# Late modulation products of a two-block mixer stack: eight half units at the entry of the gated scan instead of two

## The reference, cut to what matters

```python
c_act = jax.nn.silu(c)
for layer in range(2):
    mod = c_act @ w_ada[layer] + b_ada[layer]          # 1024 x 3072
    shift, scale, gate = mod[:, :D], mod[:, D:2*D], mod[:, 2*D:]
    h = _modulated_norm(x, norm_g[layer], shift, scale)
    ...                                                # layer 1 also: mkv = c_act @ w_ada_kv + b_ada_kv
    x = x + gate * y
```

```python
L = jnp.where(strict, einsum(k_beta, k) * decay, 0.0); a_mat = L + eye(64)
sol = triangular_solve(a_mat, rhs)                      # per head and chunk
attn = jnp.where(tril, einsum(q, k) * decay, 0.0)
...
_, o = lax.scan(step, S0, ...)                          # over the 8 chunks
```

## Time and profile before

| | us |
|---|---|
| median of 3 runs | 1232.59 |
| lowest and highest | 1232.29, 1235.76 |
| the profiled execution | 1230.61 |
| its span (first to last instruction) | 1228.7 |
| TensorE busy in the span | 1176.3 (96%) |
| VectorE, ScalarE, GpSimd busy | 487.4, 538.8, 370.7 |

### The profile page before, as it was taken

The page is one execution under the profiler, slowest core; times in us unless marked ns, Lnnn a source line. Parts: engine busy times, 40 slices in busy tenths (PEclk is TensorE's granted clock), DMA queues, the critical chain, the costliest instruction groups (busy, mean ns, idle before and its releaser), DMA issues.

```text
span 1228.7 us, 21193 instructions
## 1 busy us (share of the span) xinstructions
PE 1176.3 (96%) x8874; PEld 914.7 (74%) x8874; DVE 487.4 (40%) x919; ACT 538.8 (44%) x924; POOL 370.7 (30%) x148
## 2 busy tenths in 40 slices
PE   5999999999989999999999999999999999999998
PEld 3788886677668888777765666888887777777767
DVE  4575544544324472341314553640202332231462
ACT  4232237633336343543547774333125433754430
POOL 0143343132265314344331001332144122333250
PEclk8999999999999999999999999999999999999999
DMA  9723331356650232322422100323132321324201
GB/s 318 231 69 102 102 101 37 103 188 223 208 180 2 69 103 70 102 81 91 129 69 73 26 14 1 124 89 103 34 106 84 111 78 35 103 70 155 87 1 69
DMA packets 105761, 121.14 MB, mean 99 GB/s; under 512 B 5145, under 2 KB 91705, under 8 KB 105673
## 3 DMA queue, kind: packets, MB, share of 16 engines
q1 hardware_dynamic: 101424, 116.14, 29.9%
q10 hardware_dynamic: 4248, 3.73, 1.1%
HBM read 111.47 MB, written 2.10 MB: 92 GB/s over the span
## 4 chain that ended last, share of the span: by engine, by line
PE 84%; ACT 6%; DVE 4%; issue 3%; DMA 1%; ACTq 0%; SPq 0%; POOL 0%; DVEq 0%
PE ps L2039 42%; PE ps L2846 4%; PE ps L2644 3%; PE ps L2635 2%; PE ps L2180 2%; PE ps L2085 2%; PE ps L2426 2%; PE ps L2669 2%; PE ps L2648 1%; PE ps L2778 1%; PE ps L2123 1%; PE ps L2203 1%; PE ps L2256 1%; PE ps L2731 1%; PE ps L2453 1%
## 5 line engine op out<-in xcount | busy, mean ns | idle before, releaser
L604 POOL TENSOR_TENSOR wlo<-raw,whi 128x2048 fp32r<-128x2048 f32 x53 | 245.1, 4624 | 586.1 <-ACT whi L768 571.5
L768 ACT ACTIVATE whi<-raw 128x2048 fp32r<-128x2048 f32 x52 | 99.3, 1911 | 203.2 <-PE ps L2039 164.2
L610 POOL TENSOR_TENSOR wlo<-raw,whi 128x2048 fp32r<-128x2048 f32 x10 | 46.4, 4641 | 111.0 <-ACT whi L857 62.7
L1277 ACT ACTIVATE p<-sc,nmx 128x256 f32<-128x256 f32 x64 | 32.0, 501 | 49.6 <-PE ps L2765 29.5
L857 ACT ACTIVATE whi<-raw 128x2048 fp32r<-128x2048 f32 x11 | 21.1, 1918 | 62.7 <-PE ps L2039 62.7
L2039 PE MATMUL ps<-hC_hi,whi 128*128 128x512 f32 x184 | 47.1, 398 | 0.8 <-POOL wlo L604 0.8
L1861 DVE CUSTOM_DVE_ANT_0 sc<-ps,biast 128x256 f32<-128x256 f32 (+1 forms) x64 | 23.1, 394 | 62.2 <-PE ps L2756 33.3
L2039 PE MATMUL ps<-hC_lo,whi 128*128 128x512 f32 x184 | 45.5, 390 | 0.0
L2039 PE MATMUL ps<-hC_hi,wlo 128*128 128x512 f32 x184 | 45.4, 389 | 0.0
L2039 PEld LDWEIGHTS ps<-hC_hi,whi 128*128 128x128 f32 x184 | 33.8, 188 | 14.9 <-issue 6.4
L2039 PEld LDWEIGHTS ps<-hC_lo,whi 128*128 128x128 f32 x184 | 34.5, 188 | 7.4
(11 more groups left out here) (514 smaller groups left out, 2822.5 us busy)
## 6 DMA issues: line engine op xcount, KB each, us to landing
raw<-in_w_in_dram SPq DMA_DIRECT2D x24, 1024.0 KB, 5.2
raw<-in_w_in_a_dram SPq DMA_DIRECT2D x16, 1024.0 KB, 5.8
raw<-in_w_ada_dram SPq DMA_DIRECT2D x8, 1024.0 KB, 5.5
late_w<-in_w_ada_dram SPq DMA_DIRECT2D x8, 1024.0 KB, 5.5
raw<-in_w_kv_dram SPq DMA_DIRECT2D x8, 1024.0 KB, 5.1
raw<-in_w_in_b_dram SPq DMA_DIRECT2D x8, 1024.0 KB, 5.3
ada_a<-in_w_ada_dram SPq DMA_DIRECT2D x4, 1024.0 KB, 10.0
ada_b<-in_w_ada_dram SPq DMA_DIRECT2D x4, 1024.0 KB, 13.2
```

The lines of the kernel that those rows point to most:

```text
L604: pool.tensor_tensor(wlo[:, s, :], raw[:, s, :], whi[:, s, :].bitcast(F32), ALU.subtract).then_inc(lo_ready, 1)
L610: pool.tensor_tensor(wlo[:, s, :], raw[:, s, :], whi[:, s, :].bitcast(F32), ALU.subtract).then_inc(lo_ready, 1)
L768: A(whi[:, s, :], raw[:, s, :], ACT.Copy).then_inc(hi_ready, 1)
L1277: A(p2[:, n % 2, 256 * e:256 * e + 256], sc2[:, n % 2, 256 * e:256 * e + 256], ACT.Exp, scale=-1.0, bias=nmx[:, grp, t, 2 * hp + e:2 * hp ...
```

## The change

The first `filler` call moves three halves between `keys_keys` and `keys_queries`, and the one behind `keys_queries` takes five halves instead of two. Nothing else is edited, but `fill` is one list, so every later call takes halves that stand six places further on. The list is empty after the middle call of level 3 in pair 3. The end call of level 3, both calls of level 4 in pair 3 and the `filler(len(fill))` behind it find nothing: these are six halves (one, one, two and two).

```diff
             for h in range(2):
                 keys_keys(h)
+            filler(3)
             for h in range(2):
                 keys_queries(h)
-            filler(2)
+            filler(5)
             for p in range(HG // 2):
                 nxt = 2 * p + 2 if p < HG // 2 - 1 else None
                 for lv, b in enumerate(LEVELS):
```

## The result

The changed kernel took 1227.15 us (median of 6 runs, 1224.91 to 1227.95) beside 1232.92 us for the kernel before (1231.27 to 1237.54). The ratio is 0.9948, with an interval of 0.9928 to 0.9969: 5.8 us faster. The kernel before was 1.4 us slower in the first set (1232.92) than in the second (1231.53), and the second rests on more runs (10 and 14), so 3.3 us is the safer figure. The profiled execution took 1226.95 us with a span of 1225.0, 3.7 us less than before.

What follows compares the result with a forecast made beforehand. TensorE, busy for 1176.3 of 1228.7 us, was taken to bound the kernel. Gains of 1.5 (clock), 2.2 (end of pair 3) and 0.7 (pauses) summed to 4.4 us, giving 1228.2 us, range 1225.0 to 1233.0.

Steps and rivals of the forecast that it cites:

- The halves at the entry cost nothing: Around the key-query products: three halves ahead and five behind fit TensorE's idle time, cost 0, with 0.3 and 1.6 us spare.
- The slack of the loads: At the entry: both `late_w` loads, issued by 235.3, have landed two microseconds before 244.5, when first wanted.
- The clock, 1.5 us: Behind the entry: less idle time keeps the clock up for 28 matmuls; 1.5 us gained, from 0 to 1.6.
- The end of pair 3, 2.2 us: Levels 3 and 4 to the recurrence in pair 3: six empty calls give 0.1 + 0.0 + 0.5 + 1.5, taken as 2.2 us.
- the columns to be last before the recurrence: End of pair 3: columns with VectorE's addition need 1.02 us, ScalarE's taking out of w 0.81, so the columns stay last.
- The pauses, 0.7 us: TensorE's instruction waits, 245 to 350 us: shifted block borders and fewer late loads gain 0.7 us net, within 4 us either way.
- The sum, 4.4 us: Whole kernel: clock 1.5, end of pair 3 2.2 and pauses 0.7 give 4.4 us, a forecast of 1228.2 us.
- More pauses at the entry: Rival: four loads in a row at the entry make two more instruction portions late; 1.7 us gained, 1230.9 us; chance 0.20.
- The clock falling all the same: Rival: 1.6 us idle before the first level still drops the clock; only 2.9 us gained, 1229.7 us; chance 0.14.
- Slower: Rival: instruction blocks late in nearly all levels 2 to 4, eight more late; 5 us slower, 1237.7 us; chance 0.06.

Runs made afterwards that it cites:

- all_ahead: The changed kernel with all eight halves ahead of the key-query products and none behind; 1231.69 us, ratio 1.0004 to the kernel before.
- tail_only: The changed kernel with the six halves moved to the entry left out there but for three small matmuls; 1230.71 us, ratio 0.9996 to the kernel before.
- small_loads_before: The kernel before with late weight loads and the first output projection's load cut to an eighth; 1222.85 us beside 1231.53.
- after: The changed kernel itself, first set and first profile; 1227.15 us, ratio 0.9948 to the kernel before.
- after_again: The changed kernel measured once more, unedited, on another occasion; 1228.28 us beside 1231.53, ratio 0.9973 to the kernel before.
- even: The changed kernel with one half instead of two at the end of level 4 in every pair; 1227.56 us, ratio 0.997 to the kernel before.
- small_loads_after: The changed kernel with late weight loads and the first output projection's load cut to an eighth; 1217.39 us beside 1231.53.
- small_loads_clock: The kernel before with six spare halves in the entry's idle time and weight loads cut to an eighth; 1220.23 us, ratio 0.9904 to the kernel before.
- half_loads: paced with every late unit loaded by two 512 KB transfers instead of one of 1 MB; 1230.72 us, ratio 0.9987 to the kernel before.
- half_even: half_loads with one half instead of two at the end of level 4 in every pair; 1228.67 us, ratio 0.9978 to the kernel before.
- clock_only: The kernel before with six spare halves added in TensorE's idle time at the entry, all real halves unmoved; 1232.01 us beside 1231.22, ratio 1.000.
- paced: The changed kernel with the four loads at the entry spread out, three waiting for products of levels 0 and 1; 1230.93 us, ratio 0.9994 to the kernel before.
- ten: even with ten halves at the entry and one half instead of two ending levels 0 and 1 of pair 0; 1226.4 us beside 1231.53, ratio 0.9963.

## Why the prediction was right, step by step

**The halves at the entry cost nothing:** right. The three ahead end with 0.46 us to spare (0.3 predicted), the five behind leave 1.86 us (1.6 predicted). The slack of the loads was overrated: the text read 6 GB/s at 242 us as landed. It was the tail of a load. In the kernel before, the second of the two `late_w` loads was issued at 234.72 and landed 9.4 us later, at 244.1, where the first took 5.3 us. In all_ahead its half units waited until 244.88. In the changed kernel its load landed after 9.3 us, at some 244.4, and its half units came at 245.8; they did not wait, but it was a matter of a microsecond.

**The clock, 1.5 us:** right in size, too sure in kind. Where it holds, the distance from product to product is 3.59 us against 5.19, 1.6 us. Over all profiles:

| idle before the first level | profiles | the clock there, and the distance from product to product |
|---|---|---|
| 3.00 to 4.16 us | before, tail_only, small_loads_before, all_ahead | fell in all four, 5.0 to 6.3 us |
| 1.85 to 1.86 us | after, after_again, even, small_loads_after, small_loads_clock, half_loads, half_even | held, 3.58 to 3.59 us |
| 1.85 to 1.86 us | clock_only, paced | fell, 5.18 us |
| under 1 us, in one piece | ten | held, 3.58 us |

So the eight halves make the fall at the entry rare, not impossible, and where it falls without them it can cost 2.7 us as well as 1.6. What decides at 1.86 us stays open; full loads alone do not, for it held and fell with them.

The prediction had the clock down at the entry only, which was so in the kernel before. In five of the ten other profiles with full loads it fell in the levels too, each time behind a pause called issue:

| profile | pause before the fall | granted clock 0.50 within |
|---|---|---|
| after_again | 1.90 us | 256 to 260 us |
| clock_only | 2.25 us | 339 to 343 us |
| even | 1.60 us | 320 to 324 us |
| half_loads | 2.09 us | 277 to 281 us |
| paced | 2.10 and 2.25 us | 277 to 282 and 342 to 347 us |

The eleven profiles with full loads have 21 pauses of 1.5 to 2.5 us in the levels. Behind six of them the clock fell, behind 15 it held, one of 2.50 us among these. A fall cost 1.3 to 2.2 us, by the estimate from distance and waits. So a pause can cost nearly twice its length, and the sum of the pauses alone does not tell what they cost.

**The end of pair 3, 2.2 us:** right. Behind the w products 1.6 us came (1.5 predicted), ahead of them 0.5 (2.13 us from the last second product to w before, 1.63 after), and the middle call of level 4 gave nothing, since VectorE's 0.55 us took its place. One link was wrong: the text held the columns to be last before the recurrence, and by the chain it is ScalarE's taking out of w. ScalarE ends at 352.63 us and VectorE's addition of the columns at 352.62, so the two end together.

**The pauses, 0.7 us:** not borne out. The sum fell by 0.9 us in the first profile (8.4 to 7.5) and rose by 0.8 in the second (9.2), so that the first came near the forecast was luck. Nor did it fall for the reason given. In pair 3 there was to be one pause or less instead of 1.56 and 1.28 us. There are two, of 2.25 and 0.72 us, 3.0 in all after 2.8: the output weight's loads, now issued at 332.18 and 338.14, stand where the first falls. Levels 3 and 4 do run with the DMA at rest, from 342.75 on, as the text had it. The second pause stands in level 3 all the same: it ends at 344.91, and its 16 KB packet had moved at 342.5, with the end of the last load. This sum ranges from 4.8 to 10.0 us over the profiles with full loads, which is as much as the whole effect. What sets it in a given execution, no edit here controlled. The text bounded its change by 4 us on both sides, and all profiles lie within that.

**The sum, 4.4 us:** in the trace the recurrence came 3.96 us sooner after the key-key products (116.51 and 112.55 us). The terms measured give 1.6 + 1.6 + 0.5 + 0.9 = 4.6. Of the 0.6 us too many, 0.3 is a wait for VectorE before a second product (at 332.38) that the kernel before does not show; the rest is not assigned. In the second profile it came only 0.8 us sooner. In the runs it was 5.8 and 3.3 us, on both sides of the forecast's 4.4. The median of 1227.15 us is 1.1 below the forecast. The terms of the clock and of pair 3 were right; that the whole came out so near owes something to the pauses.

**The rivals.** More pauses at the entry: seen in after_again, 1.90 us and a fall of the clock behind it. The clock falling all the same: seen in clock_only and paced. Executions of both kinds may be what makes the second set 2.5 us poorer than the first; that is not shown. Slower: not seen with this change.

**Open:** clock_only and tail_only each gave nothing in the times (1.000, 0.9996), while the whole change gave 0.27 to 0.52%, and with small loads the parts give 2.6 and 2.8 us. The clock_only profile shows how that can be: the clock fell at the entry all the same and once more in the levels. For tail_only the profile does not show it; it was the fastest run of its set. The likeliest reading is that each part shifts the blocks of instructions against the loads in its own way and lost its 2 us in pauses and in falls of the clock behind them. That is argued from the range of both; one profile for each kernel cannot show it. Open too is which pauses the clock outlasts.

## What to carry to other kernels

Idle time of the bounding engine ahead of a dense stretch costs twice, once as idle and once as a low clock behind it; spare work belongs there first, in front of the waits that it fits under (three ahead, five behind) and not all in one place. Work taken off the end of a loop is worth what is late next, here 2.1 us for 3.2 us of halves. When small matmuls stream beside large loads, take the loads away once to see what they cost: here 9 to 11 us of 1230, some 7 of them as pauses for instructions, more than any reordering moved. And read the granted clock over the whole stretch, not only at the place of the edit.

## What was not expected of the hardware

- A pause of TensorE for instructions depends on the bytes that the DMA moves beside it: with 2.4 to 2.8 MB instead of 20.9 in 100 us the pauses went from 8.4 and 7.5 us to 0.9 and 0.5; halving the single transfers changed nothing (7.8 us). All 58 such pauses of 0.5 us or more end 2.2 to 2.8 us after a 16 KB packet of the instruction queue has moved.
- The same matmuls behind the same 1.86 us of idle TensorE kept the full clock in seven profiles and lost it in two. In the levels it fell behind six of 21 pauses of 1.5 to 2.5 us; it fell behind one of 1.60 us and held behind one of 2.50.
- Of two 1 MB loads issued one after the other, the second can have a long tail. In the kernel before they were issued at 234.30 and 234.72 us and landed after 5.3 and 9.4 us. At 242 to 243 us the DMA moved only 6 GB/s, and 11 GB/s a microsecond later, in single packets; with no other load issued in between, this was the rest of the second load and not the sign that it had landed.
